# Four residual gate rows: broadcast by DMA from a scratch row in HBM instead of by matmuls with a matrix of ones

## The reference, cut to what matters

```
mod   = silu(c) @ ada_w[l] + ada_b[l]          # for each layer l: six vectors of 1024
b1, a1, g1, b2, a2, g2 = split(mod, 6)

layer 0:  h = h + g1 * diff_attention(rms_norm(h) * (1 + a1) + b1)
          h = h + g2 * (silu(y @ w1) * (y @ w3)) @ w2          # dense, width 3584
layer 1:  h = h + g1 * (fourier_mix(rms_norm(h) * (1 + a1) + b1) @ w_o + b_o)
          h = h + g2 * mixture_of_experts(...)                  # 8 experts, 2 per token
out   = rms_norm(h) * final_g
```

## Time and profile before

| | |
|---|---|
| runs | 2679.54, 2679.96, 2680.77 us; median 2679.96 us |
| profiled execution, first to last instruction | 2681.7 us |
| PE busy | 2625.0 us, 98% of the span |
| DVE busy | 2030.9 us, 76% |
| ACT busy | 1685.6 us, 63% |
| POOL busy | 151.9 us, 6% |
| mean granted clock of TensorE | 0.992 of full speed |

### The profile page before, as it was taken

One profiled execution on the slowest core, in us unless ns is written; L12 is line 12 of the kernel. 1 busy time (PEld: TensorE's weight loads), 2 busy tenths in 40 slices (PEclk: granted clock), 3 DMA queues, 4 the chain that ended last, 5 costly groups with the idle time before them and its releaser, 6 DMA issues.

```text
span 2681.7 us, 35145 instructions
## 1 busy us (share of the span) xinstructions
PE 2625.0 (98%) x12572; PEld 2160.9 (81%) x12572; DVE 2030.9 (76%) x2363; ACT 1685.6 (63%) x2199; POOL 151.9 (6%) x196
## 2 busy tenths in 40 slices
PE   9999999999999999999999999999999999999998
PEld 7888788888888878888677888788887878888886
DVE  5557667777757765564668776799999999999998
ACT  5446654454457775453554444678788787878786
POOL 2000000000000001004210000200000000000020
PEclk9999999999999999999999999899999999999999
DMA  8555227768754338643148874699999999999996
GB/s 308 188 164 182 78 85 269 251 225 301 239 169 152 125 116 310 232 160 126 48 144 304 311 271 144 253 366 378 369 386 359 388 360 377 372 377 374 365 383 246
DMA packets 284589, 687.43 MB, mean 256 GB/s; under 512 B 13476, under 2 KB 22208, under 8 KB 284480
## 3 DMA queue, kind: packets, MB, share of 16 engines
q1 hardware_dynamic: 266208, 618.65, 64.5%
q0 software_dynamic: 18272, 67.32, 7.0%
HBM read 670.19 MB, written 15.73 MB: 256 GB/s over the span
## 4 chain that ended last, share of the span: by engine, by line
PE 86%; DVE 7%; ACT 5%; issue 2%; DVEq 0%; ACTq 0%; POOL 0%
PE ps L2561 26%; PE ps L2563 26%; PE ps L2562 25%; DVE w_lo L1636 2%; PE ps L2722 2%; ACT w_hi L876 2%; PE ps L2806 1%; DVE xt L2406 1%; DVE xn L1715 1%; DVE h L1720 1%; PE ps L3195 0%; DVE act_lo L1704 0%; ACT hp L1298 0%; PE ps L3261 0%; PE ps L2781 0%
## 5 line engine op out<-in xcount | busy, mean ns | idle before, releaser
L1636 DVE TENSOR_TENSOR w_lo<-w_raw,w_hi 128x1024 fp32r<-128x1024 f32 x1156 | 1396.0, 1226 | 423.0 <-ACT w_hi L876 392.7
L876 ACT ACTIVATE w_hi<-w_raw 128x1024 fp32r<-128x1024 f32 x1158 | 1214.0, 1059 | 754.8 <-PE ps L2563 752.3
L2561 PE MATMUL ps<-w_hi,act_hi 128*128 128x512 f32 (+1 forms) x3424 | 1343.1, 392 | 26.6 <-DVE w_lo L1636 17.5
L2563 PE MATMUL ps<-w_lo,act_hi 128*128 128x512 f32 (+1 forms) x3424 | 1321.0, 386 | 0.0
L2562 PE MATMUL ps<-w_hi,act_lo 128*128 128x512 f32 (+1 forms) x3424 | 1319.2, 385 | 0.0
L2561 PEld LDWEIGHTS ps<-w_hi,act_hi 128*128 128x128 f32 x3424 | 645.2, 188 | 171.7 <-DVE w_lo L1636 28.7
L2563 PEld LDWEIGHTS ps<-w_lo,act_hi 128*128 128x128 f32 x3424 | 645.0, 188 | 131.1
L2562 PEld LDWEIGHTS ps<-w_hi,act_lo 128*128 128x128 f32 x3424 | 645.9, 189 | 123.1 <-issue 1.4
L1627 DVE SCALAR_TENSOR_TENSOR scr<-scr,small 128x1024 f32<-128x1024 f32 x98 | 125.4, 1279 | 0.1
L1038 ACT ACTIVATE act_hi<-ps 128x512 fp32r<-128x512 f32 (+1 forms) x87 | 62.6, 720 | 71.9 <-PE ps L2722 71.9
L1762 DVE TENSOR_TENSOR act_lo<-ps,act_hi 128x512 fp32r<-128x512 f32 (+1 forms) x87 | 74.1, 851 | 39.7 <-ACT act_hi L1038 39.7
(11 more groups left out here) (516 smaller groups left out, 1424.0 us busy)
## 6 DMA issues: line engine op xcount, KB each, us to landing
w_raw<-in_moe_w SPq DMA_DIRECT2D x337, 1024.0 KB, 6.9
scr<-in_ada_w POOLq DMA_DIRECT2D x48, 1024.0 KB, 6.5
w_raw<-in_ffn_w_up SPq DMA_DIRECT2D x44, 1024.0 KB, 5.5
w_raw<-in_ffn_w_down SPq DMA_DIRECT2D x44, 1024.0 KB, 5.0
w_raw<-in_ffn_w_gate SPq DMA_DIRECT2D x43, 1024.0 KB, 5.3
w_raw<-in_ff_w SPq DMA_DIRECT2D x42, 1024.0 KB, 5.4
w_raw<-in_odd_w_in SPq DMA_DIRECT2D x20, 1024.0 KB, 5.0
w_raw<-in_even_w_in SPq DMA_DIRECT2D x14, 1024.0 KB, 5.3
```

The lines of the kernel that those rows point to most:

```text
L876: act.activation(w_hi[:, g % SPLITS, 0:c * width], w_raw[:, s % RING, o:o + c * width], ACT.Copy).then_inc(hi_done, 1)
L1636: dve.tensor_tensor(w_lo[:, g % SPLITS, 0:c * width], w_raw[:, s % RING, o:o + c * width], w_hi[:, g % SPLITS, 0:c * width].bitcast(F32), ...
L2561: pe.matmul(out_ap, hi, whi, start=start, stop=False)
L2563: return pe.matmul(out_ap, hi, wlo, start=False, stop=stop)
```

## The change

The gates go through HBM. A scratch tensor `gates` (4 rows of 1024) is added. When DVE has finished the modulation vectors of a layer (`mod_set`), POOL stores the two gates of that layer by four DMAs, each of 128 partitions x 4 columns, which lie element by element in the destination (`gates_stored`). Later POOL loads one row into `wbc`, broadcast to 128 partitions (`gate_row`), four times, each at a point of its own program; DVE waits for the landing (`gate_row_in`). The diagonals, the matmuls with ones and the copies out of PSUM go, and with them the `row` variant of `gated`: the dense feed-forward takes the order of the others.

```
+            def gates_stored(l):
+                pool.wait_ge(mod_set, l + 1)
+                for k, g in enumerate((MOD_G1, MOD_G2)):
+                    for c in (0, 4):
+                        row = gates[2 * l + k, P * c:P * (c + 4)].rearrange("(c p) -> p c", p=P)
+                        pool.dma_start(row, modv[:, g + c:g + c + 4], allow_slow_non_contiguous=True).then_inc(gates_out, 16)
+                n(gates_out, 64)
+            def gate_row(row):
+                pool.wait_ge(gates_out, n.last(gates_out))
+                pool.dma_start(wbc[:], gates[row].partition_broadcast(P)).then_inc(gate_in, 16)
+            gates_stored(0)
             for u in range(TB * DA_HEADS):
                 ...
+            pool.wait_ge(da_at, TB * DA_HEADS)
+            gate_row(0)
             pool.wait_ge(h_ready, n(h_ready))
+            gate_row(1)
             pool.dma_start(f_g, ...)                       # tables, then modulation(1)
...
             pool.wait_ge(mod_red, CTX_EVICTED + len(SUMS_DENSE))
+            gates_stored(1)
             pool.dma_start(fnb, ...)
             pool.dma_start(fin_g, ...)
+            pool.wait_ge(h_ready, n(h_ready))
+            gate_row(2)
...                                                         # behind the four scatters of token rows
+            gate_row(3)
 scalar, experts:
-                act.wait_ge(bc_ready, n(bc_ready, 4))
-                act.activation(wbc[:], banks(2, 2), ACT.Copy).then_inc(ro_act, 1)
 vector, gated:
-                    elif not row:
+                    else:
                         lo_ahead(2)
-                    if row and i == 0:
-                        row_taken(4)
-            def row_diag(col, dst=sg):                      # and its four calls
-            def row_taken(bank):                            # and its three calls
+            def gate_row_in():                              # ahead of add_half in to_dense and fourier, and of fnb * wbc
+                dve.wait_ge(gate_in, n(gate_in, 16))
-                        dve.wait_ge(ro_act, 5)
+                        dve.wait_ge(gate_in, 16 * 4)
 vector, mod_columns:
-                    dve.wait_ge(diag_done, 2)
+                    dve.wait_ge(gates_out, 64)
 tensor, gated:
-                    if row and i == 1:
-                        pe.wait_ge(row_read, n(row_read))
-                    if row and i == 0:
-                        pe.wait_ge(silu_done, n.last(silu_done) + 1)
-                        row_broadcast(rowd, 4)
-                        if i or not late:                   # late = not row
-                            hidden(i)
+                            hidden(i)                       # in the branch "if i:"
-            def row_broadcast(src=sg, bank=6):              # and its three other calls
```

More of the change, by code:

```diff
@@ L211, in build_block_kernel @@
         rows_out = nc.dram_tensor("rows_out", (MAX_BLOCKS, P, DM), F32, kind="Internal").ap()
+        gates = nc.dram_tensor("gates", (4, DM), F32, kind="Internal").ap()
         pick = sb("pick", [P, 64], F32R)
@@ L263, in build_block_kernel @@
         hlo_done = sem("hlo_done")
-        diag_done = sem("diag_done")
-        bc_ready = sem("bc_ready")
+        mod_set = sem("mod_set")
+        gates_out = sem("gates_out")
+        gate_in = sem("gate_in")
         proj_out = sem("proj_out")
@@ L1752, in start, with gated @@
                 next_rstd()
-            def gated(ff, tbs=TB, beside=None, scaled=False, sums=None, windows=None, row=False, led=False):
+            def gated(ff, tbs=TB, beside=None, scaled=False, sums=None, windows=None, led=False):
                 s = steps(ff)
@@ L1789, in gated @@
                         dve.tensor_tensor(view[0], view[1], ps[:, 6:6 + tbs, 0:width], ALU.mult).then_inc(hid_done, 1)
-                    if row and i == 0:
-                        row_taken(4)
                     if windows and i in windows:
                         context_columns(windows[i]) if sums is None else column_sums(windows[i])
-                    if row and i == len(s) - 1:
+                    if sums == 1 and i == len(s) - 1:
                         mod_columns(1)
@@ L1834, in context @@
                     n(sq_done, TB)
-            def row_diag(col, dst=sg):
-                dve.tensor_tensor(dst[:].rearrange("p (c n) -> p c n", c=DC), bc_mid(ident, DC), bc(col, P),
-                                  ALU.mult).then_inc(diag_done, 1)
-            def row_taken(bank):
-                dve.wait_ge(bc_ready, n(bc_ready))
-                dve.tensor_copy(wbc[:], banks(bank, 2)).then_inc(row_read, 1)
-                dve.wait_ge(row_read, n(row_read))
+            def gate_row_in():
+                dve.wait_ge(gate_in, n(gate_in, 16))
             def to_attention(factor):
@@ L2232, in mod_columns @@
                     ins = dve.scalar_tensor_tensor(a, a, 1.0, colv[:, g + 8 * l:g + 8 * l + 8], ALU.add, ALU.mult)
-                link(ins)
+                ins.then_inc(mod_set, 1)
+                dve.wait_ge(mod_set, n(mod_set))
                 if l == 0:
@@ L2341, in fourier @@
                 lo(1)
-                row_taken(0)
                 for k in range(2):
@@ L2545, in _ @@
             to_dense()
-            row_diag(modv[:, MOD_G2:MOD_G2 + 8], rowd)
-            gated(FF2, sums=1, windows=SUMS_DENSE, row=True, led=True)
+            gated(FF2, sums=1, windows=SUMS_DENSE, led=True)
             fourier()
@@ L2709, in to_dense, with gated @@
                 gp[0] += 4
-            def gated(ff, tbs=TB, beside=None, scaled=False, closing=None, sums=None, windows=None, row=False, ready=None, led=False):
+            def gated(ff, tbs=TB, beside=None, scaled=False, closing=None, sums=None, windows=None, ready=None, led=False):
                 s = steps(ff)
@@ L2726, in chunks @@
                     return [8 + 4 * (i % 2) + k for k in range(s[i][1] // P)]
-                late = not row
                 def first_hidden(k):
@@ L2739, in gated @@
                         pe.wait_ge(mod_red, n(mod_red))
-                    if row and i == 1:
-                        pe.wait_ge(row_read, n(row_read))
                     if i or not (scaled or led):
-                        up(per, [(0, b, 4 + k) for k, b in enumerate(blocks)], first_hidden if late and i == 1 else None,
+                        up(per, [(0, b, 4 + k) for k, b in enumerate(blocks)], first_hidden if i == 1 else None,
                            ready=None if i else ready)
@@ L2775, in gated @@
                 down(rest[4:], final=True, tbs=tbs)
-            def row_broadcast(src=sg, bank=6):
-                pe.wait_ge(diag_done, n(diag_done))
-                for i in range(2):
-                    ins = pe.matmul(ps[:, bank + i, :], ones, src[:, i * BANK:(i + 1) * BANK], start=True, stop=True)
-                ins.then_inc(bc_ready, 1)
             def even():
@@ L3472, in _ @@
             to_dense()
-            tail(gated(FF2, sums=1, windows=SUMS_DENSE, row=True, led=True))
+            tail(gated(FF2, sums=1, windows=SUMS_DENSE, led=True))
             fourier()
```

15 lines of the change are left out of this document (3 added, 12 removed).

## The result

The changed kernel takes 2686.36 us (median of 13 runs, 2683.08 to 2690.01), the kernel before 2680.57 us beside it (13 runs, 2679.38 to 2681.95). The ratio is 1.0022, 95% interval 1.0014 to 1.003: slower by 5.8 us, where 8.4 us less were forecast. The profiled execution of the changed kernel took 2685.82 us, its span is 2683.9 us, so 1.9 us lie outside the span. That makes the profiled execution of before (span 2681.7) one of about 2683.6 us, an estimate, some 3 us above its median. The two profiles therefore differ by only 2.2 us, and the stretches between fixed points say more than the spans.

The account below looks back on a forecast made before the run. PE, busy for 98% of the span, was taken as the bound; savings of 2.3 + 3.8 + 1.9 + 0.4 = 8.4 us took the runs' 2680.0 to 2671.6 us, range 2667.5 to 2677.5.

Parts of the forecast that it names:

- the price of the stores: Eight gate stores by POOL: 3.2 us each by the router load, hidden behind idle time, counted as nothing.
- upper end: Gate stores priced by the 512 KB store: 8.0 us each, 32 us for four, still hidden at both layers.
- felt store: The case that the gate stores cost time, by any amount; chance 0.07.
- The cover: Time hiding layer 1's stores and row 2's load: POOL starts at 1612.7, DVE wants the row 40 us later.
- POOL blocked by the stores: Rival: stores above some 9.5 us each turn the sign; 12 us each gives about 2699 us; felt at all, 0.07.
- Place A: Residual add behind the attention: matmuls with ones go, split starts 0.6 us earlier; 2.3 us saved, bounds 1.7 and 2.9.
- Place B: Dense feed-forward's first step: matmuls with ones, copy and split leave PE's path; 3.76 us saved, bounds 1.73 and 3.76.
- Place C: Fourier mixer, around PE's wait for the second table: matmuls go, 0.2 us of diagonal product counted; 1.9 us saved.
- Place D: Last row, made while DVE chooses the experts: only what outlasts DVE counts; 0.4 us saved, bounds 0 and 0.5.
- the clock stays low longer: Rival at the choice of experts: idle PE delays the clock's return, 3 us more, 2674.6 us; chance 0.17 with like shifts.
- The sum: Savings at the four places, 2.3 + 3.8 + 1.9 + 0.4 = 8.4 us; ends 4.1 and 10.1.

Follow-up runs that it names:

- x4: The changed kernel plus probe DMAs (stores and loads of various piece sizes) where POOL is idle; 2678.32 us in one run.
- x1: The changed kernel without layer 1's four gate stores, rows 2 and 3 loaded from rows 0 and 1; 2676.95 us, ratio to before 0.9983.
- x6: The changed kernel with gates transposed on DVE and stored in runs of 128 B, four DMAs a layer; 2677.82 us, ratio to before 0.9985.
- x8: The kernel before, with two granules split ahead in the dense feed-forward's first step, rows still made by PE; 2681.14 us, ratio 1.0.
- x10: x5 plus 7 unused products on PE at place A, where the matmuls with ones stood; 2676.84 us, ratio to before 0.9982.
- x5: The changed kernel with layer 1's gate 1 stored first and alone, row 1 loaded behind the modulation weights; 2676.34 us, ratio to before 0.998.
- x11: The kernel of x5 run again beside x10; 2676.17 us, ratio to before 0.9983.
- x12: The changed kernel with row 1 loaded behind layer 1's modulation weights, run for a profile; 2681.05 us in one run.
- x7: x6 with row 1 and the four table loads moved behind layer 1's modulation weights; 2677.7 us, ratio to before 0.9982.
- x2: The changed kernel, layer 1 reordered: two 512 KB loads, gate 1's stores, row 2's load, gate 2's stores; 2677.41 us, ratio to before 0.9987.
- x9: The changed kernel plus 40 unused products on PE where it waits for the late row; 2687.58 us, ratio to before 1.0021.

## Why the prediction was wrong, step by step

**The step that failed is the price of the stores.** The prediction took 3.2 us each from the router load, 8.0 us each as the upper end from the store of 512 KB, and counted nothing in either case. They take 10.8 us to land and hold POOL 9.5 to 12.1 us each. At layer 1 the forecast's upper end was 32 + 4.3 = 36.3 us from the first store to the row's landing; it took 54.4 us (1607.93 to 1662.29): 36.4 to the fourth issue, 9.9 for its landing, 0.5, and 7.5 for the row's load. The wait that was forecast as none is DVE's 16.95 us, and PE's 9.77 us behind it. Both bounds were rows of the wrong kind: one a load, the other a store of long runs. Neither has many small writes into one stretch of HBM, which all the dear stores of x4 share. The measured price is a third above the upper end, and with no term for a felt store the range had no room for it. Forecast and measurement lie 14.2 us apart (8.4 less, 5.8 more); in the profiles the late row's 12.6 and the 1.9 missing at B are that, within 0.3.

**The cover was mis-measured too, but by less.** "DVE wants row 2 at 1652.87" and "POOL starts at 1612.7" are times of the kernel before. The change takes work away ahead of both: DVE wanted the row at 1645.44, 7.4 us earlier, and POOL started at 1607.93, 4.8 us earlier. The cover was 37.5 us, not 40.2; the upper end's 36.3 would still have fitted, with 1.2 us to spare. A third slip is in the order: the row needs two of the four stores and stood behind all four, and with it the two 512 KB loads, which DVE wants at the same place and for which the forecast had no line.

**The rival "POOL blocked by the stores" was the right engine with the wrong place.** Its price per store was about right (it turned the sign at 9.5 us each); its 12 us each gave 2699 because it counted four full prices at both layers. Before the attention's root stand only three gaps between issues and four issues, 9.51 + 10.04 + 10.59 + 3.1 = 33.3 us against 32.99 of cover, so layer 0 cost nothing; layer 1 cost 12.57 us in the profile and 9.4 to 10.5 us by the runs (x1). A felt store had a chance of 0.07, too little beside a bound that was only the nearest row.

**The rule that the prediction cites** spoke against this part, and rightly. The Trainium skill, *DMA: Bandwidth & Descriptors*, Rules for kernel authors, tells to rearrange a strided last dimension; x6 does that, by a turn of 0.21 us on DVE, and the trace agrees with the rule: 1.6 us to landing instead of 10.8. The number of elements alone isn't the price, though: the same 512 elements take 3.2 us as a load and 5.5 us as a store 4 KB apart (x4).

**Place A, 2.3 us: right.** From ACT's copy in the attention (L1437 before) to the `add_half` at A before takes 65.87 us and x8 65.84, the ten profiles without the row matmuls 63.51 to 63.56. x10, with 1.6 us of products in their place, takes 65.22: what is left is the 0.6 us of the split. That the whole 3.85 us between the two profiles are A's would be a misreading: the copy itself, ahead of all that the change touches but the first stores, stands at 1308.2 to 1309.3 in the six profiles with a granted clock of 0.89 from 5 to 20 us (the changed kernel's among them) and at 1309.9 to 1310.7 in the seven with 0.77 (before's among them).

**Place B, 3.76 us: too high.** It gives 1.81 us in the changed kernel and 2.8 to 2.9 us (x5, x11, x12) with row 1 out of the way. The forecast let DVE's 6.45 idle us take up the later modulation weights; DVE then waited 4.00 us for them, with splits queued behind. The 512 KB of row 1 cost about 1 us of the 1.95 that are missing, and the other 1.0 is the half clock behind A, which no part of the sum had. With both out of the way (x10) B gives 3.91 us, so the working of this term was right, and what failed is that it let DVE's idle time cover the later weights and had no half clock.

**Place C, 1.9 us: right, where the clock holds.** 13.85 to 11.92 us, 1.93 less. But nine of the thirteen profiles (x1, x4, x5, x7 to x12) have a stretch of some 3.5 us at half clock between 1632 and 1640.5. The windows of x2 and x11:

```profile
1630.00:1640.00 10.00, 8.04 (x47) 7.01 (x46) 5.45 (x10) 5.36 (x13) 1.29 (x2) 1.00 0.82 220
...
1630.00:1640.00 10.00, 8.08 (x42) 7.12 (x43) 3.39 (x9) 5.20 (x12) 1.37 (x2) 0.83 0.94 229
```

It costs 1.69 us: from the first `add_half` at C to that of `experts` the profiles without a late row take 38.28 us without it (x2, x6) and 39.95 to 39.97 with it (x1, x5, x7, x10, x11); with the row matmuls it is 40.22 without (before) and 41.91 with it (x8). So x5 and x11 keep 0.25 us of C's 1.93. What brings it no run isolates.

**Place D, 0.4 us: between 0.05 more and 0.3 less** (x2, x6, x11), too small to be told apart from the clock. PE has its gap of 3.03 us. The rival that the clock stays low longer here didn't come: the stretch at 0.50 lasts 14 us before (1678.5 to 1692.5), as long in x2, x6 and x11, 10.5 us in the changed kernel, whose D is 1.60 us shorter with it, and 7 in x8.

**The sum.** A 2.3, B 2.9, C 1.9 make 7.1 us for the best order. The runs give 5.3 and 5.5 (x5, x11). The 1.69 us of half clock at C, which both their profiles have and before's hasn't, are the rest: 7.1 - 1.7 = 5.4. In the same way x1's stretches give 2.3 + 1.95 + 0.25 = 4.5, its runs 4.7. x2 and x6, whose profiles don't have that stretch, give 6.0 and 6.2 by their stretches and 4.3 and 3.8 by their runs; that fits if most of their executions have it, which only profiles of them could show. How often it comes, in them and in before, stays open.

## What to carry to other kernels

Price a DMA by a row with the same direction and the same size of runs at the far end; where there is none, say that the price is open, and don't take the largest transfer as an upper bound. Before an extra transfer is called hidden, move both the time at which it can start and the time at which its result is wanted by what the change saves ahead of them, and put behind each store only what needs it. A store of a column per partition is worth a turn on chip first, into runs that are long in HBM.

## What the runs showed of the hardware

- From the issue by POOL to landing, a store of 128 single elements into one 512 B of HBM takes 9.7 us, of 512 elements into four such stretches 11.4 us, of 512 elements 4 KB apart 5.5 us, of 32 runs of 128 B 1.6 us. The load of the same 512 elements takes 3.2 us.
- POOL issues the next such store only about when the last one has landed: idle times of 7.9 to 12.1 us put down to "issue", without any wait in the program (the changed kernel, x4, x12). Two loads of 512 KB behind the last store are issued at once, but land 14.2 and 15.4 us later in the changed kernel, 9.6 and 9.9 in x12, against 4.3 and 5.0 before.
- The time that PE stands still is not all that a wait costs. In 9.77 us of idle PE the granted clock fell to 0.50 at about 1660 and stayed there for some 10 us, 5.3 of them with work; with products in the place (x9), or a wait of 1.48 us (x12), it was 1.00. The Trainium skill, *TensorE: Matmul & The Clock Gate*, Why this matters for your kernels, warns that gaps between bursts of matmuls bring the clock down, and the trace agrees at this place.
- With 1.7 us of matmuls at A removed, a stretch of some 3.5 us at half clock stands some 20 us behind their place in every one of ten profiles, and in none of the three with matmuls there (before, x8, x10). A like stretch at C comes in nine profiles of thirteen, in x8 with the row matmuls too, and costs 1.69 us.
